# Latent attention: inverse sums enter the turn of the exponentials as a diagonal factor

## The reference, cut to what matters

```python
scale = (MLA_NOPE + MLA_ROPE) ** -0.5          # 64 and 32
s = (jnp.einsum('bqhd,bkhd->bhqk', qn, k_nope).astype(jnp.float32)
     + jnp.einsum('bqhr,bkr->bhqk', qr, k_rope).astype(jnp.float32)) * scale
p = jax.nn.softmax(s, axis=-1)
return jnp.einsum('bhqk,bkhd->bqhd', p.astype(v.dtype), v)      # v is 64 wide
```

## Time and profile before

| | us |
|---|---|
| three runs | 2895.59, 2900.49, 2895.69 (median 2895.69) |
| profiled execution, its own time | 2900.64 |
| span in the profile, first to last instruction | 2898.8 |
| mean granted TensorE clock over the span | 0.933 |
| first turn to the end of the last values, first layer | 463.8 to 534.1 |
| the same, second layer | 1049.3 to 1123.5 |

### The profile page before, as it was taken

One profiled execution on the slowest core, in us unless ns is written; L12 is line 12 of the kernel. 1 busy time (PEld: TensorE's weight loads), 2 busy tenths in 40 slices (PEclk: granted clock), 3 DMA queues, 4 the chain that ended last, 5 costly groups with the idle time before them and its releaser, 6 DMA issues. The chain is left out here.

```text
span 2898.8 us, 44918 instructions
## 1 busy us (share of the span) xinstructions
PE 2565.8 (89%) x19022; PEld 2062.8 (71%) x19060; DVE 1543.2 (53%) x2236; ACT 941.9 (32%) x1397; POOL 237.2 (8%) x208
## 2 busy tenths in 40 slices
PE   8999899989998999799667888699999882899998
PEld 7888675668886756588556776578878751788876
DVE  3474468854744678625456565555542367454522
ACT  4223125432231244332433332243322322333321
POOL 0000000110000001200233221100002000100011
PEclk9999999989999999799798999889999996899999
DMA  3332222423231223223010001133321211223231
GB/s 132 96 100 88 96 97 97 175 69 100 95 95 70 97 111 151 80 95 96 22 58 3 3 3 39 58 102 101 109 102 68 80 39 36 77 91 102 86 120 49
DMA packets 56105, 238.20 MB, mean 82 GB/s; under 512 B 6560, under 2 KB 7328, under 8 KB 47328
## 3 DMA queue, kind: packets, MB, share of 16 engines
q1 hardware_dynamic: 55904, 235.30, 23.4%
HBM read 231.08 MB, written 4.19 MB: 81 GB/s over the span
## 5 line engine op out<-in xcount | busy, mean ns | idle before, releaser
L341 PE MATMUL banks<-b_h,pin_pair 128*128 128x512 f32 x2304 | 528.3, 390 | 0.0
L341 PEld LDWEIGHTS banks<-b_h,pin_pair 128*128 128x128 f32 x2304 | 431.1, 188 | 88.9
L341 PE MATMUL banks<-ffh,ff_pair 128*128 128x512 f32 x2016 | 457.3, 389 | 0.0
L341 PEld LDWEIGHTS banks<-ffh,ff_pair 128*128 128x128 f32 x2016 | 378.4, 188 | 78.5
L341 PE MATMUL banks<-b_h,pab_pair 128*128 128x512 f32 x792 | 183.3, 394 | 8.0 <-DVE pab_pair L327 8.0
L341 PEld LDWEIGHTS banks<-b_h,pab_pair 128*128 128x128 f32 x792 | 150.5, 190 | 39.7 <-DVE pab_pair L327 8.2
L531 DVE SCALAR_TENSOR_TENSOR ada_acc<-ada_ring,sc,ada_acc 128x256 f32<-128x256 f32 x336 | 154.1, 526 | 0.0
L2680 DVE TENSOR_TENSOR ff<-ff_c,ff 128x512 fp32r<-128x512 f32 x44 | 30.5, 693 | 204.8 <-ACT ff L2668 203.4
L327 DVE TENSOR_TENSOR pin_pair<-pin_raw,pin_pair 128x1024 fp32r<-128x1024 f32 x50 | 61.3, 1226 | 140.8 <-ACT pin_pair L320 140.8
L1134 DVE SCALAR_TENSOR_TENSOR x<-banks,modf,x 128x512 f32<-128x512 f32 x32 | 24.0, 751 | 203.7 <-PE banks L359 203.7
L327 DVE TENSOR_TENSOR pin_pair<-first,pin_pair 128x1024 fp32r<-128x1024 f32 x50 | 61.3, 1226 | 125.3 <-ACT pin_pair L320 125.3
(11 more groups left out here) (508 smaller groups left out, 4511.5 us busy)
## 6 DMA issues: line engine op xcount, KB each, us to landing
ada_ring<-in_ada_w SPq DMA_DIRECT2D x48, 1024.0 KB, 7.9
ff_raw<-in_ffn_up SPq DMA_DIRECT2D x58, 512.0 KB, 3.6
pin_raw<-in_w_in SPq DMA_DIRECT2D x50, 512.0 KB, 3.5
first<-in_w_in SPq DMA_DIRECT2D x48, 512.0 KB, 3.4
dn_raw<-in_ffn_down SPq DMA_DIRECT2D x16, 1408.0 KB, 6.0
first<-in_ffn_up SPq DMA_DIRECT2D x30, 512.0 KB, 3.5
pab_raw<-in_ab_in SPq DMA_DIRECT2D x23, 512.0 KB, 3.5
out_raw<-in_w_out SPq DMA_DIRECT2D x12, 512.0 KB, 9.0
```

What stands on the lines that cost most here:

```text
L341: mm = nc.tensor.matmul(bank, w(a, k), x(b, k), start=k == 0 and i == 0, stop=k == kt - 1 and i == 2)
```

## The change

The exponentials stay as they are. DVE multiplies the identity, 128x128, by the inverse sums instead, which gives a diagonal matrix for each head of the unit; `flip(u)` is now an ordinary product of the exponentials (stationary, as before) with that diagonal (moving), in place of a transpose by the identity. The result in PSUM is the same: turned exponentials, each query's column scaled by its inverse sum. The diagonals lie in the tile `spread`, which is free by then, in two slots. From unit 2 on, DVE waits for `flipped` of the unit two before, whose diagonal it overwrites.

```diff
@@ mla_attention
         tmp, inv, spread = sb("tmp", [P, T]), sb("inv", [P, T]), sb("spread", [P, TT, P])
+        diag = spread[:].rearrange("p (u e) n -> p u e n", u=2)
@@ flip(u), on PE
                         for j in range(TT):
-                            mm = nc.tensor.transpose(m.ps[:, 4 + e, j * P:j * P + P],
-                                                     ex[:, 2 * (u % 2) + e, j * P:j * P + P], m.ident[:])
+                            mm = nc.tensor.matmul(m.ps[:, 4 + e, j * P:j * P + P],
+                                                  ex[:, 2 * (u % 2) + e, j * P:j * P + P], diag[:, u % 2, e],
+                                                  start=j == 0, stop=j == TT - 1, skip_group_check=True)
                         mm.then_inc(flipped, 1)
@@ the units, on DVE
                     chain.step(nc.vector.reciprocal(total[:, u % 2], total[:, u % 2]))
                     for e in range(2):
-                        nc.vector.tensor_scalar(ex[:, s + e], ex[:, s + e], total[:, u % 2, e:e + 1], None, ALU.mult)\
-                            .then_inc(evened, 1)
+                        if u >= 2:
+                            dve.wait_ge(flipped, 2 * u + e - 3)
+                        nc.vector.tensor_scalar(diag[:, u % 2, e], m.ident[:], total[:, u % 2, e:e + 1], None,
+                                                ALU.mult).then_inc(evened, 1)
```

## The result

| | before | after |
|---|---|---|
| median (lowest to highest) | 2895.99 (2895.59 to 2900.49, 4 runs) | 2923.11 (2919.05 to 2926.26, 4 runs) |
| span of the profiled execution | 2898.8 | 2921.7 |
| its mean granted clock | 0.933 | 0.938 |

The change makes the kernel 27.1 us slower: ratio 1.0081, 95% interval 1.0065 to 1.0096. Repeated on another chip, with six runs beside 23 of before, the ratio was 1.0079 (1.0052 to 1.0106). The forecast was 2920.7, slower. Two single executions, 3890.73 us of the kernel with the turn in f32r and 3858.14 us of the one with half of it in f32r, ran at a mean granted clock of 0.63 and 0.64 and are left out of all medians, means and ratios here.

A forecast was written before the change was run, and what follows sets the result against it. The prediction took PE to bound the units, ACT's copies following within a tenth. Per layer 12.6 + 0.9 - 0.8 - 0.2 = 12.5 us, two layers 25.0, so the median 2895.69 becomes 2920.7; range 2914 to 2929.

The forecast's parts named there:

- PE is the bound in the units: Units of latent attention: PE alone needs 4.18 us of a mean period of 4.24, ACT's copies following within a tenth.
- DVE's multiplication is off the path: In the units, L1039 has 0.9 us of slack before the turn; PE waits for it only before the first turn.
- A product is two records where a transpose is one, 0.111 apart: In the turn, 8 records become 16 per unit, each 0.111 us, as read from L899 and L852.
- the transpose mode four times faster for FP32: Rival in the turn: a product costs four transposes, 2.7 us extra per turn, about 2974; chance 0.02.
- 0.90 per turn: Each unit's turn gets 0.90 us longer on PE; turns 0 to 13 pay in full, 12.6 us per layer.
- Turn 14 free: Next-to-last turn of a layer: its 0.90 us goes into the 2.18 us its values wait for the copies.
- turn 15 at 0.9: Last turn of a layer: everything up to its values hangs on it, so it pays 0.9 us.
- waits for the copies back with 0.8: In the units, PE's waits for ACT's copies go, about 7 per layer of 0.12 us: -0.8 per layer.
- start 0.2: Unit 0, where PE waits for DVE's multiplication: the first head's half shrinks, -0.2 us per layer.
- Sum 25.0: Both layers of the units together: 12.5 us slower per layer, 25.0 us in all.
- The clock: Rival: half-clock stretches around the units move between layers, giving +19.3 us (2915.0) or, the other way, 2926.4; chance 0.15.
- the prediction's own sign of being wrong: In the profile after, stretches at half clock moving by more than 5 us would show the prediction wrong.

The follow-up runs named there:

- PE's part alone: Kernel before with the turn as a float32 product with the identity, DVE still multiplying the exponentials at 128x512: median 2925.13 beside 2904.25, ratio 1.007.
- DVE's part alone: Changed kernel with the transposes of before, DVE making the 128x128 diagonals: median 2901.62 beside 2904.25 for the kernel before, ratio 0.9996.
- doubling: Changed kernel with each head's four products done twice, 32 records a turn: 2985.4, ratio 1.0276 to the kernel before.
- halving: Changed kernel with products for head 0 of each pair only, head 1 turned by transposes, 12 records a turn: ratio 1.0041 to the kernel before.

## Why the prediction was right

- *PE is the bound in the units; DVE's multiplication is off the path.* Right in what it was used for: PE's part alone costs the whole, DVE's part alone nothing. PE alone needed 4.16, not 4.18. Incomplete in one respect: DVE's loop was level with PE's, which the prediction did not see, because it measured slack only toward the waiting turn. It did not matter, as the change took work off DVE.
- *A product is two records where a transpose is one, 0.111 apart.* Right: 512 records in place of 256 over both layers, 0.112 apart (a transpose's 0.109). The page TensorE: Matmul & The Clock Gate of the Trainium skill (Terms: the transpose mode four times faster for FP32) does not hold for this: doubling, halving and the row of L899 all give a factor of two.
- *0.90 per turn.* It was 0.96 from a turn's start to the scores. The term was made of 8 x 0.111 and almost nothing for the first 8 records; eight records at 0.112 are 0.90, the first step of a turn is 0.05 longer (0.213 for 0.165), and the 0.002 to 0.003 by which products stand further apart than transposes add 0.01 to 0.02. Against the period of 4.18, in which 0.02 was a wait, it is 0.94; the sum had 0.90, and over 28 turns that is 1.1 us.
- *Turn 14 free, turn 15 at 0.9, waits for the copies back with 0.8, start 0.2.* Turn 14: 4.30 before and after. Turn 15: 0.91. The waits went, six in the first layer and not seven. The start: PE's wait 4.4 to 4.2.
- *Sum 25.0.* The stages give 26.6 (2 x 13.50 - 0.4), the runs at equal clock 27.2 +- 0.8, the medians 27.1 and, on the other chip, 23.6.
- *The clock.* Given 0.15, in either direction, and up to 5.7 us. It is there, in part: the profiled execution alone would have said +22.9, and its stretches moved past the prediction's own sign of being wrong, while the medians did not follow. That the medians of the first comparison (27.1) agree with the stages (26.6) to half a microsecond is partly luck: on the other chip they are 23.6 apart. The span of the single runs of before went from 2889 to 2915 us with the mean clock from 0.939 to 0.928, a wider spread than the three runs first shown let one expect.

## What to carry to other kernels

Before an operand of a PE transpose is given a second duty, count matmul records: a float32 transpose is one, a float32 product two, each 0.11 us at 128 moving columns with a stationary tile of its own, and it is paid in full where PE is the bound. Folding a scaling into a product is only worth it if the engine that is relieved ends the wait; measure its slack both toward whoever waits for the result and toward what stands behind it on its own queue. And look at the granted clock before believing one execution: here it moved the difference by 4 us in one profile, and a change of operand form by a hundred.

## What the hardware showed that was not expected

With the turn in f32r the granted clock stayed at 1.2 GHz for 133 and 160 us with PE busy nearly all the time, in both layers, and came back with the next stage or as soon as half of the turn was float32. An f32r record of 128 moving columns that follows a weight load of its own took 0.213 us at half clock and 0.110 to 0.112 at full clock, as long as a float32 transpose. In the kernel before L911's f32r records of 512 columns stand 0.23 apart at full clock:

```profile
443.53 5.70 PE L911 MATMUL banks<-mla_low,mla_ukv 128*128 128x512 f32 x24
```

(5.70 less a last duration of 0.39, over 23.) That is four times the columns in the time of two such records: at 128 columns f32r had no advantage.
